# Moving the low weights of a streamed two-part float matmul by 64 bytes in on-chip memory

## The reference

```python
z = h @ w_in[i]
y = jnp.concatenate([y_a, y_b, y_c, y_d], axis=-1) @ w_o[i]
x = x + y
uf = causal_dwconv(rmsnorm(x, g_ffn[i]) @ w_up[i], w_ffn_conv[i])
x = x + (jax.nn.silu(gate) * up) @ w_down[i]
pe_gate = jax.nn.sigmoid(rmsnorm(x, g_pe[i]) @ w_pg[i])
...
h = rms_norm(x, norm_g)
p = split_columns(jnp.einsum("bsd,de->bse", h, w_in))
return x + jnp.einsum("bse,ed->bsd", mixed, w_out)
```

## The kernel before

| tensor | begins at | modulo 512 | step from one slot or tile to the next |
|---|---|---|---|
| `H` (streams) | 32896 | 128 | 2048 a tile |
| `raw`, `wlo` | 65984 | 448 | 8192 a slot, 512 a weight tile |
| `whi` | 98944 | 128 | 8192 a slot, 512 a weight tile |
| `pT_hl` (streams) | 149312 | 320 | 2048 a tile |
| `z`, `G` (streams) | 179840 | 128 | 2048 a tile of `G` |
| `cq` (streams) | 212608 | 128 | 2048 a tile |

## Time and profile before

### The profile page before, as it was taken

The page is one execution under the profiler, slowest core; times in us unless marked ns, Lnnn a source line. Parts: engine busy times, 40 slices in busy tenths (PEclk is TensorE's granted clock), DMA queues, the critical chain, the costliest instruction groups (busy, mean ns, idle before and its releaser), DMA issues. The chain is left out here.

```text
span 3350.2 us, 53769 instructions
## 1 busy us (share of the span) xinstructions
PE 3327.6 (99%) x20366; PEld 2929.1 (87%) x20366; DVE 2617.8 (78%) x3394; ACT 1531.6 (46%) x1642; POOL 864.2 (26%) x633
## 2 busy tenths in 40 slices
PE   9999999999999999999999999999999999999998
PEld 8989888888888989888888888888888888888897
DVE  8897788787786888887887787867867866678865
ACT  5644444343433556544443434335444444445443
POOL 0422432121122423414332121214432004150004
PEclk9999999999999999999999999999999999999999
DMA  6445555555555554455555555555544455544454
GB/s 241 148 163 176 189 188 189 178 202 177 206 174 189 203 182 165 151 176 187 190 188 178 198 180 199 180 190 200 193 164 153 167 173 189 180 164 151 167 185 151
DMA packets 90647, 605.21 MB, mean 181 GB/s; under 512 B 10192, under 2 KB 10352, under 8 KB 29296
## 3 DMA queue, kind: packets, MB, share of 16 engines
q1 hardware_dynamic: 89424, 599.83, 52.0%
q10 hardware_dynamic: 1056, 3.11, 0.2%
HBM read 600.80 MB, written 2.10 MB: 180 GB/s over the span
## 5 line engine op out<-in xcount | busy, mean ns | idle before, releaser
L642 PE MATMUL bank<-H,whi 128*128 128x512 f32 x6496 | 1574.3, 393 | 1.5 <-DVE z L1661 1.5
L1164 ACT ACTIVATE whi<-raw 128x2048 fp32r<-128x2048 f32 (+2 forms) x609 | 1093.6, 1796 | 1044.6 <-DMA raw<-in_slabs_down 259.8
L1630 DVE TENSOR_TENSOR wlo<-raw,whi 128x2048 fp32r<-128x2048 f32 (+2 forms) x609 | 1328.4, 2181 | 243.2 <-ACT whi L1164 233.1
L642 PEld LDWEIGHTS bank<-H,whi 128*128 128x128 f32 x6496 | 1188.7, 188 | 238.6 <-issue 5.9
L653 PEld LDWEIGHTS bank<-H,wlo 128*128 128x128 f32 x6624 | 849.1, 188 | 34.3
L653 PE MATMUL bank<-H,wlo 128*128 128x256 f32 x6624 | 871.1, 281 | 0.0
L511 POOL TENSOR_TENSOR sqtmp<-tmp 128x256 f32<-128x256 f32 x88 | 218.9, 2488 | 867.8 <-DVE tmp L2211 867.8
L642 PE MATMUL bank<-G,whi 128*128 128x512 f32 x1408 | 343.0, 391 | 0.0
L642 PEld LDWEIGHTS bank<-G,whi 128*128 128x128 f32 x1408 | 255.4, 188 | 48.0
L1564 ACT ACTIVATE G<-sqtmp 128x256 f32 (+1 forms) x88 | 36.8, 418 | 404.0 <-POOL sqtmp L511 404.0
L489 POOL TENSOR_TENSOR sqacc<-sqacc,sqtmp 128x256 f32<-128x256 f32 x119 | 199.4, 1676 | 9.4
(11 more groups left out here) (390 smaller groups left out, 2881.4 us busy)
## 6 DMA issues: line engine op xcount, KB each, us to landing
raw<-in_slabs_up SPq DMA_DIRECT2D x176, 1024.0 KB, 4.8
raw<-in_slabs_down SPq DMA_DIRECT2D x128, 704.0 KB, 4.0
raw<-in_slabs_wo SPq DMA_DIRECT2D x32, 1024.0 KB, 4.8
raw<-in_slabs_pg SPq DMA_DIRECT2D x32, 1024.0 KB, 4.9
raw<-in_slabs_gates SPq DMA_DIRECT2D x32, 1024.0 KB, 4.9
raw<-in_slabs_wout SPq DMA_DIRECT2D x32, 1024.0 KB, 4.8
raw<-in_slabs_sc SPq DMA_DIRECT2D x24, 1024.0 KB, 4.8
raw<-in_slabs_fox SPq DMA_DIRECT2D x24, 1024.0 KB, 4.9
```

The costliest lines, as they stand in the source:

```text
L642: pe.matmul(b[0:r.m, :], whi[:, n % RAW, w], r.src[:, k, :], start=at == 0, stop=False)
L1164: act.activation(whi[:, n % RAW, 0:w], raw[:, n % RAW, 0:w], ACT.Copy).then_inc(S("hi_ready"), 1)
L1630: dve.tensor_tensor(wlo[:, n % RAW, 0:w], raw[:, n % RAW, 0:w], whi[:, n % RAW, 0:w].bitcast(F32), ALU.subtract).then_inc(S("lo_ready"), 1)
```

## The change

`ahead_of_raw` shrinks from 80 floats (320 bytes) to 64 (256 bytes), and `ahead_of_whi` grows from 48 floats (192 bytes) to 64 (256 bytes). So `raw` and `wlo`, which are one memory, begin 64 bytes lower, at 65920 (384 modulo 512); `whi` and all that follows it stay where they were. The distance of `wlo` to `H`, `G` and `cq` becomes 256 (it was 192), and to `pT_hl` 64 (it was 128). The distance of `raw` to `whi`, which ACT and DVE go through side by side, becomes 256 (it was 192). Every engine's list of instructions is the same as before, in number and in order; only addresses differ.

```diff
     x = sb("x", [P, DC, T])
     H = sb("H", [P, DC, 2 * T], F32R)
-    sb("ahead_of_raw", [P, 80])
+    sb("ahead_of_raw", [P, 64])
     area_raw = nc.sbuf_tensor("raw", [P, RAW, 2048], F32)
     raw = area_raw.__enter__()
     area_raw.__exit__(None, None, None)
     wlo = sb("wlo", [P, RAW, 2048], F32R)
-    sb("ahead_of_whi", [P, 48])
+    sb("ahead_of_whi", [P, 64])
     whi = sb("whi", [P, RAW, 2048], F32R)
```

## The result

| | before | after |
|---|---|---|
| median of 6 runs each, us | 3352.75 (3349.70 to 3353.93) | 3363.96 (3362.18 to 3368.70) |
| ratio to before, 95% interval | | 1.0035 (1.0025 to 1.0045) |
| profiled execution, its span, us | 3352.41, 3350.2 | 3363.42, 3361.2 |

The changed kernel is slower by 11 us. The forecast of no change was wrong; the rival "the low step goes to 120 ns" is what happened. The page after shows the same picture as the earlier trace rows: the matrix engine is the bound, at full clock, and its busy time grew by 12 us.

What follows compares the result with a forecast made beforehand. The prediction took the sum of PE's matmul steps, at full clock, to bound the kernel. Its four parts, each 0, summed to 0, leaving 3351.3 us against the median; the range was 3320 to 3377 for 8 in 10.

Steps and rivals of the forecast that it cites:

- no change: Chosen case: the low step stays within 1 ns of 118 ns, 3351 us; chance 0.32.
- the low step goes to 120 ns: Rival in every low block: each low matmul pays 2 ns, as at distance 0; +20 us, 3371 us; chance 0.20.
- a partial gain: Rival: some low blocks reach the fast step, or 116 ns instead of 118; 3335 us; chance 0.20.
- Parts 3 and 4: DVE's subtraction and ACT's rounding through `raw` and `whi`, and transfers into `raw`: 0 us, hidden by slabs of cover.
- Part 1: Low weights against the stream, 8032 matmuls of line 653, distance 192 to 256: 0 us, ends -40 and +16 us.
- the mixes: Retention and `pT_hl` matmuls with loads at several distances, steps of 118 and 117.5 ns; basis for 0 us in low blocks.
- the repeat of 256 bytes: Argument for the 120 ns rival: a pattern repeating every 256 bytes would make distance 256 the same as 0.
- part 2: Low weights as the stream, line 677, 320 matmuls in value slabs, distance 192 to 256: 0, 1 us either way.
- The low blocks fall into the fast step: Rival: low blocks settle at 113 ns also after a full high block; 33 us gained, 3318 us; chance 0.12.

Runs made afterwards that it cites:

- e1: Kernel before with everything but the low weights up by 64 bytes, so high and low weights at offset 0 as in the changed kernel: 3366.46 us, 1.0047.
- e2: Kernel before with low weights 64 bytes above the streaming tiles instead of 320, high weights unmoved: 3352.86 us, 1.0001.
- e4: Kernel before with high and low weights both moved to offset 64 modulo 256 from the streaming tiles: 3354.76 us, 1.0008.
- e6: Kernel before with high and low weights both moved to offset 192 modulo 256 from the streaming tiles: 3342.00 us, 0.9972.
- e13: Kernel before, same addresses, with the last high matmul of each block issued as two of 256 columns: 3357.91 us, 1.0013.
- e14: e6 with the last high matmul of each block issued as two: 3345.49 us, 0.9973 of the kernel before.
- e10: Kernel before with high weights at offset 192 and low weights at 0, modulo 256 from the streaming tiles: 3366.16 us, 1.0043.
- e9: Kernel before with high weights at offset 192, low weights at 64, modulo 256 from the streaming tiles: 3364.15 us, 1.0038.
- e8: Kernel before with only the low weights moved, to 32 bytes above the streaming tiles: 3362.65 us, 1.0034.
- e3: Kernel before with only the low weights moved, to 128 bytes above the streaming tiles: 3370.29 us, 1.0058.
- e12: Kernel before with only the low weights moved, to 224 bytes above the streaming tiles: 3348.00 us, 0.9989.
- e5: Kernel before with only the low weights moved, to 192 bytes above the streaming tiles: 3364.54 us, 1.0043.

## Why the prediction was wrong

The measured 3364 us lies inside the stated range of 3320 to 3377, and 0.37 stood on slower. But the range held a partial gain, no change and a step of 120 ns alike, so it says nothing for the case that was chosen, no change.

**What bounds the kernel** was right: PE's steps and nothing else; clock, waits, DVE, ACT and the transfers stayed as they were. Parts 3 and 4 of the sum, at 0, held, and so did the high blocks' 2.52 us and line 596, at offset 0 in both: its steps are 120 ns before and after.

**Part 1 failed: "The value I take is 0, because the mixes, the rows nearest in kind to "another distance for the low load", don't move from 118."** It cost 12.4 us on line 653: the low step went from 117.7 to 119.4 ns, outside the 117 to 119 that the prediction gave as its own limit. The mixes are averages over loads at different offsets, and I read their agreement as "addresses don't matter". The row with one offset alone was the earlier trace rows, 120 ns at offset 0, and I set it aside as an end of the range. It was the measurement: with the repeat of 256 bytes that I named as a rival, 256 is 0 and the step 120. Two readings before contradicted "addresses don't count", 120 against 113 ns for 256 columns with one weight load each; I took their spread for an uncertainty instead of a dependence to be explained. What the trace of before couldn't give is the period, which e1 and e2 showed.

**The rival's size.** It said +20 us; line 653 cost 12.4. The entry keeps the first two steps of a block at 113 and 119 ns, so a block of 16 pays 1.913 - 1.887 = 26 ns, not 16 x 2 = 32. The blocks that had been at 113 pay 1.90 - 1.83 = 0.07 us, not 16 x 7 ns = 0.11 us. And the value slabs gave 3.0 us back. In part 2 I had counted only the 320 matmuls in which `wlo` streams past `H`, at 1 us either way; their neighbours got faster too, 960 matmuls in all.

**The other rivals.** "The low blocks fall into the fast step" isn't what this change does, but it exists: e4 has it in most blocks. There the high blocks took it back, a coupling that no part of the prediction had.

**The rule of the Trainium skill** ("TensorE: Matmul & The Clock Gate", "Step-by-step: what each phase is for"), by which loading the next weights takes nothing from the running matmul, does not agree with this kernel: the `pT_hl` steps are 113 ns in the changed kernel and 120 ns in e6, with the same instructions and another offset between the two operands. The rule's 0 us was also the forecast; the measurement decides. The figure of N / 2.4 GHz + 2.5 ns from the same page ("Wait — 56ns, not 53.3ns?"), by which I estimate 109.2 ns for 256 columns, was reached by no steady fp32r block in these runs; the lowest was 113.

**What stays open.** That the stationary and the streaming read meet in the memory is inferred from the dependence on their offset and its period; no run shows the memory itself. And while e13 and e14 show that the entry picks among steady steps, no way was found to put every block into the 113 ns: e13 only lost six fast blocks, and e14 only changed which blocks are fast.

## What to carry to other kernels

Where PE is the bound at full clock with weights changed for every matmul, the address of the stationary tile less that of the streaming tile, modulo 256 here, is worth a sweep in steps of 32 or 64 bytes: the span between the best and the worst kernel of this case is 1.4%. Read it from single steps of blocks with one offset, not from averages or mean durations, and sweep the high and low weights together, since a gain in one kind of block was taken back in the next one (e4). "Farther apart" is no guide while the period isn't known.

## What the runs showed of the hardware

- The step of fp32r matmuls of 256 columns with a new weight tile each depends on the offset modulo 256. It is 120 ns at 0 (changed kernel, e1, line 596 everywhere; in the down projection of e10 it goes round 117, 118 and 120), and 113 or 118 at 64 and 192 (before, e4, e6, e9). Offset 320 is the same as 64 (e2). At 32, 128 and 224 beside high weights at 0 it goes round several values, 112 to 124 ns (e8, e3, e12).
- With 512 columns it settles at 227 ns at offset 0, after five steps of 228 to 236 (before). At 64 it alternates between 231 and 236, or stays at 233 in half of the down slabs (e4). At 192 it goes round 226, 229 and 232 (e6, e10) or stays at 233 (the slabs of 16 in e9).
- A block has more than one steady step at the same addresses. In e6, 250 of 524 full low blocks are at 113 ns and the others at 118, mostly in turn, and the split matmul of e14 changes 254 of them. In e13 it moves six blocks from 113 to 118 ns.
- The address of one buffer moves the time of matmuls that don't read it: with only the low weights moved, line 642 takes 14 us more in e5 and 2.5 us less in e3.
